# A decoder layer on one core: ScalarE rounds the first two gate tiles inside its last head, and the barrier before the output projection goes

## The reference

```
proj = h @ w_in            # attention q/k/v | HGRN2 f,i,q,g | memory q | 3 gates of 1024 columns
A: dilated sliding-window attention, 3 groups, merged by log-sum-exp weights
B: HGRN2 gated linear recurrence        C: attention into 256 memory tokens
mix = (sum_g sigmoid(gate_g) * (branch_g @ w_branch_g)) @ w_out
h = LN(alpha*h + mix);  h = LN(alpha*h + PEER(h))      # PEER: product-key experts, 8 heads, top 16
```

## Time and profile before

| what | value |
|---|---|
| time, median of 3 runs (lowest, highest) | 4051.45 us (4048.8, 4055.97) |
| the profiled execution: time / span in the trace | 4052.45 / 4050.6 us |
| its mean granted TensorE clock | 0.958 |
| busy, share of the span: PE / DVE / POOL / ACT | 91% / 66% / 39% / 31% |
| DMA, mean over the span | 280 GB/s |

### The profile page before, as it was taken

How to read it: one execution, slowest core, us unless ns; L and a number is a source line. 1 busy time by engine, 2 the same in 40 slices (tenths; PEclk the granted TensorE clock), 3 DMA queues, 4 the chain that set the end, 5 groups by cost and what they waited for, 6 DMA issues and landing times.

```text
span 4050.6 us, 45984 instructions
## 1 busy us (share of the span) xinstructions
PE 3694.7 (91%) x14431; PEld 2458.7 (61%) x14431; DVE 2655.6 (66%) x5440; ACT 1235.9 (31%) x2640; POOL 1577.4 (39%) x1341
## 2 busy tenths in 40 slices
PE   6999989898888979867779999898999999999998
PEld 5778768677777768656444454453544545445763
DVE  1445542248777766666999889889877868743540
ACT  1333332222333232224342240330412404224530
POOL 2556534331222157655344443444444444410000
PEclk8999999999999989988889999999999999999999
DMA  7666633346777658878999999999999999963567
GB/s 244 202 226 221 214 101 96 98 154 238 240 222 233 221 183 261 276 237 316 320 379 400 380 394 377 375 378 376 399 401 392 401 410 397 396 256 127 185 204 268
DMA packets 506327, 1133.97 MB, mean 280 GB/s; under 512 B 41180, under 2 KB 250508, under 8 KB 505904
## 3 DMA queue, kind: packets, MB, share of 16 engines
q1 hardware_dynamic: 335120, 570.94, 40.5%
q0 software_dynamic: 147456, 536.94, 35.4%
q10 hardware_dynamic: 23584, 24.12, 1.7%
HBM read 1044.81 MB, written 89.41 MB: 280 GB/s over the span
## 4 chain that ended last, share of the span: by engine, by line
PE 34%; DVE 14%; DMA 3%; issue 2%; ACT 1%; DVEq 0%; ACTq 0%
PE ps L1391 27%; DVE u_ring L2400 5%; PE ps L1377 4%; PE ps L1423 2%; DMA u_ring<-in_peer_u,pidx 2%; DVE split_v L2447 1%; DMA v_ring<-in_peer_v 1%; ACT split_v L1847 1%; DVE hot L2392 1%; DVE hot L2393 1%; DVE inds_own L1961 0%; DVE got_own L2006 0%; DVE inds_own L1949 0%; DVE left_own L1952 0%; ACT split_c L1846 0%
## 5 line engine op out<-in xcount | busy, mean ns | idle before, releaser
L1391 PE MATMUL ps<-v_ring,table 128*128 128x512 f32 x3584 | 1593.0, 595 | 17.4 <-DMA v_ring<-in_peer_v 17.2
L994 POOL DMA_INDIRECT u_ring<-in_peer_u,pidx x800 | 775.1, 969 | 935.6 <-DVE coefe L2400 881.6
L1391 PEld LDWEIGHTS ps<-v_ring,table 128*128 128x128 f32 x3584 | 663.9, 191 | 772.9 <-issue 725.1
L2400 DVE CUSTOM_DVE_ANT_0 u_ring<-u_ring,h_up 128x1024 f32<-128x1024 f32 x800 | 948.2, 1217 | 137.4 <-DMA u_ring<-in_peer_u,pidx 126.5
L1053 PE MATMUL ps<-x_hi,w_hi 128*128 128x512 f32 x1280 | 516.8, 404 | 39.2 <-ACT w_hi L1499 23.6
L1056 PE MATMUL ps<-x_lo,w_hi 128*128 128x512 f32 x1280 | 506.7, 396 | 0.0
L1377 PEld LDWEIGHTS ps<-hot,hot 128*128 128x128 f32 x2048 | 282.2, 203 | 157.0 <-issue 111.1
L938 POOL TENSOR_TENSOR w_lo<-w_raw,w_hi 128x1024 fp32r<-128x1024 f32 x120 | 300.7, 2511 | 197.0 <-ACT w_hi L1499 192.2
L1815 ACT ACTIVATE table<-ps 128x512 f32<-128x512 f32 (+3 forms) x256 | 229.3, 896 | 435.8 <-PE ps L1377 435.8
L1803 ACT ACTIVATE hot<-hot,by_slot 128x128 f32<-128x128 f32 x1024 | 321.2, 388 | 75.7 <-DVE hot L2392 71.0
L959 POOL DMA_INDIRECT e_ring<-in_peer_u,icole x224 | 229.8, 1026 | 274.1 <-DVE dotse L2058 196.2
(11 more groups left out here) (326 smaller groups left out, 4184.7 us busy)
## 6 DMA issues: line engine op xcount, KB each, us to landing
v_ring<-in_peer_v SPq DMA_DIRECT2D x576, 512.0 KB, 6.8
w_raw<-in_w_in SPq DMA_DIRECT2D x88, 512.0 KB, 5.0
wh_d<-w_hi SPq DMA_DIRECT2D x56, 512.0 KB, 2.6
wl_d<-w_lo SPq DMA_DIRECT2D x56, 512.0 KB, 4.0
w_hi<-wh_d SPq DMA_DIRECT2D x56, 512.0 KB, 4.5
w_lo<-wl_d SPq DMA_DIRECT2D x56, 512.0 KB, 4.7
u_ring<-in_peer_u,pidx POOLq DMA_INDIRECT x800, 9.2
raw_mid<-in_w_branch SPq DMA_DIRECT2D x48, 256.0 KB, 3.3
```

The source lines that it names most:

```text
L994: pool.indirect_dma_start(out=u_ring[:, slot_of(n, k), :], out_offset=None, in_=u_tab, in_offset=bass.IndirectOffsetOnAxis(ap=pidx[n % 2][ ...
L1391: last = pe.matmul(ps[2 * (n % 2) + c][:, :], table[:, row_of(n, i1), :], v_ring[:, j % V_TILES, HALF * c:HALF * c + HALF], start=(n == p ...
L2400: dve.tensor_tensor_reduce(out=u_ring[:, slot_of(n, k), :], in0=u_ring[:, slot_of(n, k), :], in1=h1_up[:, :, :].rearrange("p c n -> p (c n)"),
```

## The change

1. On ACT the body of the head loop becomes a function `act_head(h, last)`; the loop runs over three heads and the fourth is written out behind it. In that one the rounding of gate tile (0,0) stands behind the stores of group 2 (`spill(2)`), and that of (0,1) behind the last copies of attention values (`values_out(2)`), ahead of the exponential of the merge. Behind the loop neither is left.
2. The barrier `boundary(hf, 2)` is gone on PE, ACT and DVE, and the later ones are numbered one lower in each half. Instead, PE waits for the sigmoids s0 and s1 of the last column block (the output tiles go to the same banks) and for `m_lo` of the second last one, and the first pair of output tiles is written out with a wait for the last `m_lo` only before its last block of the contraction (`whole`).
3. SP's `load_ln` waits for the last gated matmul of PE instead of the barrier.

```diff
@@ -667,7 +667,7 @@
         def boundary(hf, k):
-            return 2 + 6 * hf + k
+            return 2 + 5 * hf + k - (k > 2)
...
@@ -782,7 +782,7 @@
             def load_ln(hf):
-                sp.wait_ge(stage, 3 * boundary(hf, 2))
+                sp.wait_ge(MP.sem, MP.after("B2", KD * hf + KD - 1))
...
@@ -1042,7 +1042,7 @@
-            def tile(n, hi, lo, k_n, out, ready=False):
+            def tile(n, hi, lo, k_n, out, ready=False, whole=None):
...
@@ -1050,6 +1050,8 @@
                 for k in range(k_n):
+                    if whole is not None and k == k_n - 1:
+                        pe.wait_ge(*whole)
                     first = pe.matmul(out, w_hi[b][:, k, :], hi[:, k, :], start=(k == 0), stop=False)
...
@@ -1311,18 +1313,23 @@
-                cross(pe, boundary(hf, 2))
-
-
-                with pe.Fori(0, KD // 2) as e:
+                def out_pair(e, whole):
+
                     it = KD // 2 * hf + e
                     for t in range(2):
                         pe.wait_ge(OA.sem, OA.after(f"c{t}", it - 1))
-                        tile((t, t0 + T_OUT // 2 + e), m_hi, m_lo, KD, ps[t][:, :]).then_inc(*OP.mark(f"O{t}"))
+                        tile((t, t0 + T_OUT // 2 + e), m_hi, m_lo, KD, ps[t][:, :], whole=whole).then_inc(*OP.mark(f"O{t}"))
...
+                for t in range(2):
+                    pe.wait_ge(MA.sem, MA.after(f"s{t}", KD * hf + KD - 1))
+                pe.wait_ge(MV.sem, MV.after("lo", KD * hf + KD - 2))
+                out_pair(0, (MV.sem, MV.after("lo", KD * hf + KD - 1)))
+                with pe.Fori(1, KD // 2) as e:
+                    out_pair(e, None)
...
@@ -1540,7 +1547,11 @@
-                with act.Fori(0, NH) as h:
+                def mid_hi(j, t):
+                    weight_hi(t % 2, t0 + T_MID // 2 + NT_MID // 2 * j + t // 2, mid_raw(hf, j, t), MID_K[t])
+
+                def act_head(h, last):
+
                     it = NH * hf + h
...
@@ -1688,6 +1699,8 @@
                     copy("vn2", v_n[:, 2, :], job("Tv2")[:, :])
                     spill(2)
+                    if last:
+                        mid_hi(0, 0)
                     p("p1p")
...
@@ -1704,6 +1717,8 @@
                     values_out(2)
+                    if last:
+                        mid_hi(0, 1)
                     v("md")
...
@@ -1712,12 +1727,12 @@
                     if hf == 1:
                         head_stored(h)
+                with act.Fori(0, NH - 1) as h:
+                    act_head(h, False)
+                act_head(NH - 1, True)
...
@@ -1728,8 +1743,6 @@
-                for t in range(2):
-                    mid_hi(0, t)
                 cross(act, boundary(hf, 1))
                 mid_hi(0, 2)
...
@@ -1741,7 +1754,6 @@
-                cross(act, boundary(hf, 2))
...
@@ -2304,7 +2316,6 @@
-                cross(dve, boundary(hf, 2))
```

More of the change, by code:

```diff
@@ L1717, in _ @@
                         act.wait_ge(spilled[g], 32 * NH + 32)
-                def mid_hi(j, t):
-                    weight_hi(t % 2, t0 + T_MID // 2 + NT_MID // 2 * j + t // 2, mid_raw(hf, j, t), MID_K[t])
                 def mid_gates(j):
```

## The result

The changed kernel took 4026.82 us (median of 6 runs, 4022.15 to 4034.01), the one before 4052.3 us (6 runs, 4042.63 to 4059.6). The ratio is 0.9938, 95% interval 0.9925 to 0.995: 25 us faster, between 20 and 30. I had predicted 4016.6 us, 35 us faster, with 4026.0 as the upper end. The direction was right, the size was not: the time lies just outside the range, and 10 of the 35 us did not come. A later set of runs gave 4028.4 us and 0.9943 (0.993 to 0.9957).

The account below looks back on a forecast made before the run. Up to about slice 19 PE was taken as the busiest engine, dipping where stages end. Savings of 10.06 + 12.55 + 4.7 + 7.5 = 34.8 us from 4052.45, less 1.0, gave 4016.6 us; range 4010 to 4026.

Parts of the forecast that it names:

- Part 1, both places A: End of the last head, both halves: two ScalarE roundings moved into idle gaps start gate tiles earlier; 10.06 and 12.55 us.
- Part 2, half 0: Gates to output projection: without the barrier PE runs 14 matmuls, waits 1.9 us for `m_lo`, keeps clock, gains 4.7 us.
- Part 2, half 1: Gates to output projection: POOL's split and gathers come 8.6 us earlier; 7.5 us gained, ends 4 and 8.6.
- The early load: Rival, half 1 output projection: residual's load delays last gathers, `m_lo` 3.9 us late; gain there 0 to 3; chance 0.13.
- The head stage: Head stage of half 1, up to the last head: predicted gain 0 us.
- My signs of being wrong: ACT idle before new roundings; longer head stages; fourth dot over 2 us later; 0.77 us matmuls behind half 0's new wait.
- not early: Rival, last head: raw gate tiles missing, ACT blocks, the moved roundings gain nothing, 4039; chance 0.08, including half failing.
- slower by fresh code: Rival, written-out last head: some 130 more ACT instructions per half each stall; 4060 at 0.17 us each; chance 0.03.

## Why the prediction was wrong, step by step

- **Part 1, both places A: right.** 10.06 and 12.55 predicted, 9.8 to 10.1 and 12.3 to 12.6 measured. The roundings went into the gaps of ScalarE that I had named, DVE was ready 1 us ahead of PE. Alone this part measured 20 us of 22.6.
- **Part 2, half 0: mechanism and size right, one term open.** The wait was 1.94 us (1.9 predicted), the chain to `m_lo` 5.01 (5.03). I let the clock stay up because it had behind 2.52 us. One row was not enough: of the seven traces with this wait of 1.94 us the ten matmuls took 2.40 us in five and 3.98 us in two. Against the first trace of the kernel before, the gain is 4.5 or 2.9.
- **Part 2, half 1: the failed step.** I took 7.5 us and got 0.4 to 1.2 (2.6 at most, against the highest trace with the barrier): most of the 10 us that did not come. The step was: POOL's split and gathers can come 8.6 us earlier, PE has 7.9 us of slack, so up to 7.9 us can come through. POOL did start 8.6 us earlier. But I gave the dot products behind `m_lo` only the gathers to wait for, and put DVE's wait for the residual's load, which stands ahead of them in its queue, at nothing. In the kernel before it was next to nothing: gather and load landed within 0.6 us of each other. After the change the gathers were early, the load landed 19.5 us behind the last gated matmul, and DVE's first dot stood at 19.9 instead of 21.0. With the load and its wait out of the way the stretch took 85.8 us, 6.7 to 7.2 less than before: close to my 7.5, so that what I had said of POOL and PE holds once that wait is gone.
- **The early load.** This collision I had as a rival, priced at 0 to 3.9 us on `m_lo`; it measured 4.0. In time it cost 2 us of the stretch, the wait 4. The rival's half 1 (0 to 3 us) was the one that came, and 0.13 was too low a chance. My argument against it, that the gathers are issued before the load, fails for the last of them (1650.65 against 1650.60). Nor was my main range drawn from my own ends: they gave 4013.3 to 4023.7, and I wrote 4010 to 4021. The Trainium skill (DMA: Bandwidth & Descriptors, section Queues, rings and completion order) has each DMA engine take turns between the queues it has work for. The traces agree as far as they show it: beside the load the third dot started 2.1 us later and the fourth 4.0, and the load took 13.0 instead of 8.1 us.
- **The head stage and the rest.** Another 2.6 to 5.9 us of the miss stand in the head stage of half 1, which I had put at nothing; its cause is open. The expert phase behind varied by 11 us between two traces of the same kernel (first to last matmul of L1398, the changed kernel: 2079.1 and 2068.3 us), which is why the medians of kernels that differ by 3 us should not be ranked.
- **My signs of being wrong.** Two came: the fourth dot more than 2 us later (4.0), and slow matmuls behind the new wait in half 0, in two traces of seven.
- **The rivals** on ScalarE (not early; slower by fresh code) fell as expected. One number in the second was wrong: I took 130 more instructions per half, but the listing's difference (1770 - 1641 = 129 rows) is that of both halves together. Each would have had to cost 34.8 / 129 = 0.27 us to undo the gain, not 0.13.

The best versions are the change with DVE's wait moved to the sum (4019.0) and the change with the load in four parts and both tiles first (4018.0), each some 8 to 10 us faster than the change as it stands.

## What to carry to other kernels

When a barrier goes, ask of each engine behind it what the next wait is, in the order of its queue, and compare an operation's start with the landing of every transfer that it waits for, not only with the one that the profile names as the last. A wait for a bulk load belongs directly ahead of the first instruction that reads it: one placed ahead of a loop also holds back work that only shares the queue. Where two waits end together, removing one shows nothing of the other: ask for the second too before counting on the first. Sending a load earlier moves its bytes into someone else's stretch; price it by what is in flight at that moment. Sending it later holds back whatever stands behind it in the same DMA queue.

## What was unexpected of the hardware

The same wait of 1.94 us on PE, in the same place, was followed by the 1.2 GHz level in two traces and by 2.4 GHz in five: a term for the clock behind a wait of about 2 us needs both values. Once the load, the gathers and the weights overlapped, DMA moved 364 GB/s over 20 us with its engines fully busy, and a load of 2 MB went from 8.1 to 13.0 us, one of 512 KB sent behind it from 11.2 to 18.5. The kernel's time scattered from 4022 to 4034 us in one set, more than the difference between several of the versions tried.
